# Attention of the shorter sequence in pairs of units: one maximum, one reciprocal and one copy for two

## What is computed

```python
sc = einsum('bqhcd,bkhcd->bhcqk', q_blk, k)      # c = 0, 1: two score maps for each head
p = softmax(sc, axis=-1)
w = p[:, :, 0] - lam * p[:, :, 1]
o = einsum('bhqk,bkhe->bqhe', w, v)              # then an RMSNorm over each head's 128 columns
```

## Time and profile before

| | |
|---|---|
| median of 3 runs | 2004.49 us (2004.25 to 2005.94) |
| the profiled execution | 2006.16 us, span 2004.4 us |
| TensorE, DVE, ACT, GpSimd busy | 93%, 74%, 53%, 24% of the span |
| mean granted clock of TensorE | 0.966 of full speed |
| attention of the short sequence | from 863.7 to 931.1 us of the span |

### The profile page before, as it was taken

The page is one execution under the profiler, slowest core; times in us unless marked ns, Lnnn a source line. Parts: engine busy times, 40 slices in busy tenths (PEclk is TensorE's granted clock), DMA queues, the critical chain, the costliest instruction groups (busy, mean ns, idle before and its releaser), DMA issues.

```text
span 2004.4 us, 31667 instructions
## 1 busy us (share of the span) xinstructions
PE 1871.2 (93%) x11554; PEld 1667.6 (83%) x11554; DVE 1480.8 (74%) x2246; ACT 1061.6 (53%) x1528; POOL 487.5 (24%) x366
## 2 busy tenths in 40 slices
PE   6999998998899989987995999999999999999995
PEld 6888876887579988766795999999999999999994
DVE  5335877996877568976757777877777777877786
ACT  4233337885671433375633555556555555556564
POOL 3444333221860133332501100111111100111110
PEclk9999999998999989988987999999999999999998
DMA  5332320000023423300335777777777777777886
GB/s 204 102 120 100 107 77 33 1 1 1 22 71 151 176 87 112 98 12 1 116 128 209 228 243 260 242 265 258 261 246 245 237 243 263 243 261 263 284 276 243
DMA packets 62755, 325.13 MB, mean 162 GB/s; under 512 B 8336, under 2 KB 14608, under 8 KB 32464
## 3 DMA queue, kind: packets, MB, share of 16 engines
q1 hardware_dynamic: 46640, 265.55, 37.3%
q0 software_dynamic: 16032, 58.47, 9.9%
HBM read 287.55 MB, written 34.87 MB: 161 GB/s over the span
## 4 chain that ended last, share of the span: by engine, by line
PE 76%; DVE 13%; ACT 5%; issue 4%; POOL 1%; DMA 1%; SPq 0%; POOLq 0%; DVEq 0%; ACTq 0%
PE psum L2386 20%; PE psum L1973 9%; PE psum L2387 9%; PE psum L1975 9%; PE psum L1974 9%; DVE conv_acc L1423 3%; PE psum L2409 3%; PE psum L2408 3%; PE psum L2124 3%; PE psum L2103 2%; PE psum L2112 1%; PE psum L2104 1%; PE psum L2240 1%; ACT prob L984 1%; PE psum L2328 1%
## 5 line engine op out<-in xcount | busy, mean ns | idle before, releaser
L2386 PE MATMUL psum<-xT,whi 128*128 128x384 f32 x1024 | 295.7, 361 | 1.3 <-DVE xT L1949 1.3
L2386 PE MATMUL psum<-xT,whi_x 128*128 128x384 f32 x1024 | 293.7, 360 | 0.0
L1878 DVE TENSOR_TENSOR wlo_x<-wraw_x,whi_x 128x2048 fp32r<-128x2048 f32 x96 | 218.4, 2288 | 59.0 <-ACT whi_x L1199 59.0
L2387 PE MATMUL psum<-xT,wlo 128*128 128x192 f32 x1024 | 257.8, 252 | 0.0
L2387 PE MATMUL psum<-xT,wlo_x 128*128 128x192 f32 x1024 | 256.8, 251 | 0.0
L1973 PE MATMUL psum<-ht_hi,whi 128*128 128x512 f32 (+1 forms) x624 | 238.6, 382 | 19.4 <-POOL wlo L597 7.0
L1975 PE MATMUL psum<-ht_hi,wlo 128*128 128x512 f32 (+1 forms) x624 | 236.0, 378 | 0.0
L1974 PE MATMUL psum<-ht_lo,whi 128*128 128x512 f32 (+1 forms) x624 | 235.9, 378 | 0.0
L1878 DVE TENSOR_TENSOR wlo<-wraw,whi 128x2048 fp32r<-128x2048 f32 x94 | 213.6, 2284 | 16.2 <-ACT whi L1199 16.2
L597 POOL TENSOR_TENSOR wlo<-wraw,whi 128x2048 fp32r<-128x2048 f32 x36 | 167.8, 4662 | 220.4 <-ACT whi L824 220.4
L2387 PEld LDWEIGHTS psum<-xT,wlo 128*128 128x128 f32 x1024 | 197.5, 193 | 0.6
(11 more groups left out here) (378 smaller groups left out, 4343.4 us busy)
## 6 DMA issues: line engine op xcount, KB each, us to landing
wraw<-moe_chunks SPq DMA_DIRECT2D x96, 1024.0 KB, 5.8
wraw_x<-moe_chunks SPq DMA_DIRECT2D x96, 1024.0 KB, 6.3
wraw<-w_in_chunks SPq DMA_DIRECT2D x36, 1024.0 KB, 4.9
wraw<-w_out_chunks SPq DMA_DIRECT2D x8, 1024.0 KB, 6.1
xin<-x POOLq DMA_DIRECT2D x12, 512.0 KB, 4.8
acc_scratch<-x POOLq DMA_DIRECT2D x12, 512.0 KB, 3.2
h_scratch<-h POOLq DMA_DIRECT2D x12, 512.0 KB, 3.9
fin<-acc_scratch SPq DMA_DIRECT2D x11, 512.0 KB, 11.3
```

Of the source, the lines that this page charges most:

```text
L1878: tt(moe_lo[i % 4], moe_raw[i % 4].rearrange("p (k n) -> p k n", k=KT), moe_hi[i % 4].bitcast(F32), ALU.subtract).then_inc(w_lo_done, 1)
L2386: mm(bank[:, 0:2 * TOK], hi[:, k, cols], xT[:, k, :], start=(k == 0), stop=False)
L2387: last = mm(bank[:, 0:TOK], lo[:, k, cols], xT[:, k, 0:TOK], start=False, stop=(k == KT - 1))
```

## The change

In the short sequence a step is now a pair of neighbouring units of one head (`each = 2`), 8 steps instead of 16; the long sequence is as before (`each = 1`). The helper `steps(s)` gives units in a step, number of steps, steps in a query block and steps in a head. A pair's two maps for c = 0 take both 512-column halves of the 1024 columns of PSUM that the long sequence uses, and so do those for c = 1.

A pair has one maximum of 128x1024 to 128x2 for each c, four exponentials of 512 columns as before (each has its own bias and its own sum), one reciprocal of four numbers, one small product for both units, two differences of 512 columns, eight transposes, one copy of 1024 columns, and the products of both units. A pair's semaphore for the scores comes after four matmuls, and the next pair's scores for c wait for both exponentials of that c.

The pieces of queries and keys are dealt out anew: the even pair of a head issues query pieces one and two, both low query pieces and both parts of the key, high and low; the odd pair issues query pieces three and four. GpSimd's low parts wait for `wg_done` only in the long sequence now. `scaled`, `squares` and `summed` come at other steps, and in the short sequence `squares` and `summed` of the last two blocks stand behind the loop, where only the last one did. `rsum` has 32 columns and another address. The dt steps keep their numbers, which now count pairs.

```diff
-        def q_low(u):
+        def q_low(s, u):
-            return (0, 1, None, None)[u % 4]
+            return ((0, 1) if u % 2 == 0 else ()) if s else ((0,), (1,), (), ())[u % 4]
+        def q_pieces(s, u):
+            if s:
+                return Q_PIECES[2 * (u % 2):2 * (u % 2) + 2]
             return (Q_PIECES[0:1], Q_PIECES[1:2], Q_PIECES[2:4], ())[u % 4]
-        def k_pieces(u, nt):
-            return [c_ for c_ in range(2) if u % nt == nt // 2 - 2 + c_]
+        def k_pieces(s, u):
+            return ((0, 1) if u % 2 == 0 else ()) if s else [c_ for c_ in range(2) if u % 8 == 2 + c_]
+        def steps(s):
+            each = 1 + s
+            return each, 4 * SEQS[s][1] // each, 4 // each, SEQS[s][1] // each
...
# GpSimd, k_lo and q_lo
-                        pool.wait_ge(wg_done, 4 * t0 + u + 1)
+                        if s == 0:
+                            pool.wait_ge(wg_done, u + 1)
...
# ACT
+                            for x_ in range(each):
+                                at_ = each * (2 * (u % 2) + c_) + x_
+                                act.activation(sl[:, c_, x_ * L:(x_ + 1) * L],
+                                               psum[:, 1024 * c_ + x_ * L:1024 * c_ + (x_ + 1) * L], ACT.Exp,
+                                               bias=ostat[:, 0, at_:at_ + 1], accum_out=ostat[:, 1, at_:at_ + 1]
+                                               ).then_inc(exp_done, 1)
-                        act.activation(wgtT[:, w % 2, 0:L], psum[:, 2048:2048 + L], ACT.Copy).then_inc(wt_out, 1)
+                        act.activation(wgtT[:, w % 2, :], psum[:, 2048:2048 + 1024], ACT.Copy).then_inc(wt_out, 1)
-                    if u // 4 + 1 < nt:
-                        q_hi(u // 4 + 1, q_pieces(u))
+                    if u // group + 1 < nt:
+                        q_hi(u // group + 1, q_pieces(s, u))
...
-                squares(act, s, nt - 1)
+                for a in range(nt - each, nt):
+                    squares(act, s, a)
...
# DVE
+                    own.link(dve.reciprocal(sums, ostat[:, 1, o2:o2 + 2 * each]))
+                    own.link(stt(out=ostat[:, 2, first], in0=ostat[:, 1, first], scalar=lamt[:, 6:7],
+                                 in1=sums[:, each:2 * each], op0=ALU.mult, op1=ALU.mult))
+                    for x_ in range(each):
+                        at_ = slice(x_ * L, (x_ + 1) * L)
+                        ins = stt(out=sl[:, 0, at_], in0=sl[:, 1, at_], scalar=ostat[:, 2, o2 + x_:o2 + x_ + 1],
+                                  in1=sl[:, 0, at_], op0=ALU.mult, op1=ALU.add)
+                    ins.then_inc(wg_done, 1)
...
+                            dve.tensor_reduce(ostat[:, 0, at_:at_ + each],
+                                              psum[:, 1024 * c_:1024 * c_ + 1024].rearrange("p (x l) -> p x l", x=each),
+                                              AX.X, ALU.max, negate=True).then_inc(mx_done, 1)
...
-                summed(nt - 1)
+                for a in range(nt - each, nt):
+                    summed(a)
...
# TensorE
+                            if u % group == 0:
+                                pe.wait_ge(qhi_done, 4 * (t0 + u // group) + c_ + 3)
+                                pe.wait_ge(qlo_done, 2 * (t0 + u // group) + c_ + 1)
...
                             if u:
-                                pe.wait_ge(exp_done, 2 * (U - 1) + c_ + 1)
-                            for q in range(L // BLK):
+                                pe.wait_ge(exp_done, 8 * t0 + each * (2 * (u - 1) + c_ + 1))
+                            for q in range(2):
+                                unit = each * u + (q if s else 0)
...
-                        for kk in range(nt):
+                        for kk in range(8):
                             last = pe.transpose(psum[:, 2048 + kk * P:2048 + (kk + 1) * P],
                                                 prob[s][w % 2][:, 0, kk * P:(kk + 1) * P], ident)
```

More of the change, by code:

```diff
@@ L625, in q_lo @@
                     h, i = (4 * a) // nt, (4 * a) % nt
[L626 to L633, removed]
+                    for c_ in q_low(s, u):
+                        if s == 0:
+                            pool.wait_ge(wg_done, u + 1)
+                        pool.wait_ge(qhi_done, 4 * (t0 + a) + Q_PIECES.index((c_, c_)) + 1)
+                        rows = slice(64 * c_, 64 * c_ + 64)
+                        pool.tensor_tensor(qhl[rows, a % 2, 2 + c_, :], qT[rows, h, i * P:i * P + BLK],
+                                           qhl[rows, a % 2, c_, :].bitcast(F32), ALU.subtract).then_inc(qlo_done, 1)
+                each, count, group, head = steps(s)
+                for u in range(count):
                     if u == 0:
@@ L638, in _ @@
                         pool.wait_ge(qlo_clear, 4 * s + 4)
[L639 to L642, removed]
+                    if u // group + 1 < nt:
+                        q_lo(u // group + 1, u)
+                    if u // head + 1 < HEADS:
+                        k_lo(u // head + 1, u)
                 pool.memset(mark[0:1, 1:2], 0.0).then_inc(phase_pool, 1)
@@ L975, in _ @@
                 use_table(ACT.Exp)
-                for u in range(4 * nt + 2):
+                each, count, group, head = steps(s)
+                for u in range(count + 2):
                     U = 4 * t0 + u
-                    if u < 4 * nt:
+                    if u < count:
                         sl = prob[s][u % 2]
@@ L1491, in dt_step @@
                         tt(grid(6), grid(5), rep(stat[:, 1, :]), ALU.mult).then_inc(dt_v, 1)
+                each, count, group, head = steps(s)
                 def weights(w):
                     W = 4 * t0 + w
-                    sl, o2 = prob[s][w % 2], 2 * (w % 2)
-                    dve.wait_ge(exp_done, 2 * W + 2)
-                    own.link(dve.reciprocal(rsum[:, 2 * (w % 8):2 * (w % 8) + 2], ostat[:, 1, o2:o2 + 2]))
-                    own.link(stt(out=ostat[:, 2, o2:o2 + 1], in0=ostat[:, 1, o2:o2 + 1],
-                                 scalar=rsum[:, 2 * (w % 8) + 1:2 * (w % 8) + 2], in1=lamt[:, 6:7],
-                                 op0=ALU.mult, op1=ALU.mult))
@@ L1502, in weights @@
-                    stt(out=sl[:, 0, 0:L], in0=sl[:, 1, 0:L], scalar=ostat[:, 2, o2:o2 + 1], in1=sl[:, 0, 0:L],
-                        op0=ALU.mult, op1=ALU.add).then_inc(wg_done, 1)
+                    sl, o2 = prob[s][w % 2], 2 * each * (w % 2)
+                    first = slice(o2, o2 + each)
+                    sums = rsum[:, 2 * each * (w % 8):2 * each * (w % 8 + 1)]
+                    dve.wait_ge(exp_done, 8 * t0 + 2 * each * (w + 1))
+                    own.link(dve.reciprocal(sums, ostat[:, 1, o2:o2 + 2 * each]))
@@ L1513, in summed @@
+                    r = rsum[:, at_:at_ + 8].rearrange("p (u c x) -> p u c x", c=2, x=each)[:, :, 0, :]
+                    tt(oatt[:, i:i + 4, h * P:(h + 1) * P].rearrange("p (u x) n -> p u x n", x=each),
+                       pb[6 + a % 2].rearrange("p (u x n) -> p u x n", x=each, n=P),
+                       r.unsqueeze(3).to_broadcast([P, group, each, P]), ALU.mult).then_inc(o_scaled, 1)
                 def summed(a):
@@ L2085, in _ @@
                 pe.wait_ge(rot_out, NR * (b + 1))
-                for u in range(4 * nt + 3):
+                each, count, group, head = steps(s)
+                for u in range(count + 3):
                     U = 4 * t0 + u
-                    if u < 4 * nt:
-                        h, i = u // nt, u % nt
+                    if u < count:
+                        h, i = u // head, u % head
                         for c_ in range(2):
```

79 lines of the change are left out of this document (35 added, 44 removed).

## The result

The changed kernel takes 2015.25 us, median of 5 runs (2013.64 to 2017.03), the kernel before 2005.19 us beside it, also 5 (2004.25 to 2005.98): 1.0050 times, with a 95% interval of 1.0035 to 1.0065. The prediction was 2013.5, range 2007.5 to 2018.5. The profiled execution took 2015.85 us, with a span of 2014.0 where before had 2004.4.

The account below looks back on a forecast made before the run. The prediction took a ring from ACT to TensorE and back, 2.80 us a unit, to bound the short attention. Its terms, 1.4 + 7.2 + 0.4 = 9.0 us on the median 2004.49, gave 2013.5 us, range 2007.5 to 2018.5.

Parts of the forecast that it names:

- The markers and the rest: Short attention's times, from first exponential 866.41 to last sum of squares 925.02; the change leaves what follows that alone.
- DVE's saving of 2.4 us at 0: Short attention: 32 maxima become 16, 2.4 us less DVE work, taken as worth 0, at most 2.4.
- the ring: Short attention's loop from ACT to TensorE and back to ACT, 2.80 us a unit, with DVE beside it.
- A free pair 5.05 us against 5.60: A short-attention pair without late waits takes 5.05 us against 5.60, one round of hand-overs for two; eight pairs 4.4 us.
- Three late waits: Scores of pairs 2, 4, 6 wait for ACT's late query copies; TensorE idles 4.7, up to 5 and 3 us.
- The walk at full clock, +1.4 us: Pair-by-pair start times at TensorE's full clock, through the tail: the last sum ends at 926.4, 1.4 us later than 925.02.
- The clock, 7.2 us and 0.4 for the products: Clock falls before pairs 2, 4, 6: 2.4 us each on scores and transposes, 7.2; products 0.4, bounds 0 and 4.8.
- GpSimd and DVE at 0: GpSimd's low halves run into DVE's differences after even pairs: about 2.5 us, hidden by slack, taken as 0, at most 4.
- Rival C: GpSimd and DVE hold each other, key's low halves late: 4 us more, low-clock products 4.8 more, 2017.5 to 2022; chance 0.11.
- Rival A: The waits are there, but TensorE's clock falls at most once: 1.4 to 4 us, 2006 to 2008.5; chance 0.17.
- Rival B: Late pieces come before TensorE asks, each pair gains 0.55 us: 4.4 less the tail's extra, at most -4, 2000.5; chance 0.04.
- The sum of 9.0 us: Predicted total loss: 1.4 from the walk plus 7.2 from the clock, 8.6, and 0.4 for the products.

Follow-up runs that it names:

- e1_even: Changed kernel with all four query pieces of the next head copied in the even pair, none in the odd one: 2008.36 us, ratio 1.0015 to before.
- e4_ahead: Changed kernel with the query pieces dealt one pair earlier, each later pair keeping its count of copies: 2005.20 us, ratio 0.9997 to before.
- e2_fill: Changed kernel with unused small identity matmuls before the scores of pairs 1, 2, 4 and 6, where TensorE idled: 2008.80 us, ratio 1.0022 to before.
- e3_poolwait: Changed kernel with GpSimd's wait for `wg_done` put back ahead of the short sequence's low halves: 2019.66 us, ratio 1.0069 to before.
- e10_atail: e4_ahead with the copy of pair 5's weights ahead of the last pair's exponentials, no small matmuls or early table load: 2003.71 us, ratio 0.9994.
- e7_afill: e4_ahead plus the exponential's table loaded right behind the logarithm and small identity matmuls before the scores of pairs 1 and 2: 2005.85 us, ratio 0.9998.
- e8_tail: e7_afill with ACT's copy of pair 5's weights ahead of the last pair's four exponentials, not behind them: 2000.12 us, ratio 0.9974 to before.
- e12_again: The kernel of e8_tail run once more, nothing else changed: 1999.93 us, ratio 0.9973 to before.

## Why the prediction was right, and where it was off

- **The markers and the rest.** All of the loss is in the stage, none of it in the rest (1945.4 and 1945.8).
- **DVE's saving of 2.4 us at 0.** Maxima of 1223 ns, DVE behind TensorE in the waits of the changed kernel, and no version shows a gain from it alone. But its ground, that the ring hides DVE, was not so in the first units of before: ACT waited 4.4 us for DVE's maxima, 2.71 of them ahead of unit 2. Not tested by itself.
- **A free pair 5.05 us against 5.60.** Pair 6 took 5.0 (48.0 to 53.0). Shown.
- **Three late waits.** 4.37, 4.33 and 3.94 us, against 4.7, up to 5 and 3. e1_even and e4_ahead took them away, and 7.0 and 10.6 us with them. Shown; the third was a little longer than forecast.
- **The walk at full clock, +1.4 us.** With the clock held (e2_fill) it is 61.6 against 60.0 predicted. The step that failed is "The reload of the exponential's table, another 1.28, fits beside TensorE's 3.1": it stood behind them, since the load starts only when the exponential's own wait is over (the 4.11 us above). Pair 4 was 1.3 us late by it, in e2_fill and after.
- **The clock, 7.2 us and 0.4 for the products.** 5.6 to 7.0 us measured, but otherwise dealt: the steps of after less those of e2_fill are 2.2 us at pair 2 (8.8 and 6.6), 0.3 at pair 3, 1.6 at pair 4 (12.0 and 10.4), 1.2 at pair 6 (9.1 and 7.9) and 1.6 in the tail (15.5 and 13.9), 7.0 together. At pair 6 the clock fell only at 911.7, one microsecond into the scores. In the tail it was the sixteen products, where the sum had 0.4 for all products. The term came out right in part by luck: the three falls that it priced at 7.2 were worth 5.1, and the two that it left out gave 1.9. "I take a fall at each" held, but there were five falls, and a walk that puts falls only at the longest idlings misses the one of the tail, after 2.15 us. No walk by idle times alone could place it, for e2_fill and e4_ahead idled as long there without a fall.
- **GpSimd and DVE at 0.** The timeline bears it out (2.8 us of slack behind the first held differences), and the hold is 1.98 us on two differences (3.39 less 1.41), where the walk had about 2.5. Rival C needed scores waiting on `khl` more than on `qhl`. In the scores' weight loads that came when the wait was put back (e3_poolwait) or the query wait was gone (e1_even, e4_ahead); it set the scores' start only in e3_poolwait.
- **Rival A**, 2006 to 2008.5 with the clock held: e2_fill is that case by force, 2008.8, just above it.
- **Rival B**, the hand-overs decide at 2000.5 when the pieces are early: e4_ahead made them early and came to 2005.2. Up to pair 7 there were 3.2 us of its 4.4, all from the first two pairs, and they were lost in the tail, which B's sum had as "4.4 less the tail's extra, at most -4": the tail's extra was 3 us (13.9 against 10.9), and should have been taken off. To reach 2000.1 it took the early copy, the small matmuls and the early load together; with the early copy alone (e10_atail) it is 2003.7.

The sum of 9.0 us stands against 9.95 in the stage and 10.1 in the medians: 1.3 by the table, 0.3 by small shifts, less 0.6 by the clock as a whole. The mechanism was right, the late query copies and the clock behind them; that the total comes so close is owed in part to errors of opposite sign.

## What to carry to other kernels

When two units are joined into one, every piece of preparation that was spread over the units must be put again: look at which instruction in an in-order queue stands behind the last piece, and for how many units' worth of work it is. Price the deeper pipeline's tail apart from its loop: with the pieces early, pair 7 started 3.2 us sooner and the tail gave 3.0 back. One copy moved ahead of four exponentials in the last pair then gave about 1 us by its order, and with small matmuls against the low clock beside it the kernel came below the one before; without them it was level (0.9994, interval 0.9983 to 1.0005). Here a wait that kept two engines from holding each other cost more than it saved, because the matmuls waited for what it delayed (e3_poolwait).

## What the runs showed of the hardware

- The length of an idling alone does not tell whether the clock falls. e7_afill and e8_tail are the same up to the last pair, with the same idlings of 2.44 us before pair 3 and 2.72 us before pair 5, some 1 us shifted; in one profiled execution the clock fell at both, in the other at none, nor in that of e12_again, the same kernel as e8_tail. First e7_afill, then e8_tail, 878 to 884 and 892 to 896:

```profile
878.00:884.00 6.00, 4.21 (x15) 3.28 (x16) 4.94 (x9) 5.64 (x13) 0.36 (x1) 0.72 0.00 1
...
892.00:896.00 4.00, 1.75 (x4) 1.46 (x5) 3.63 (x9) 3.95 (x11) 2.52 (x2) 0.73 0.00 0
```
```profile
878.00:884.00 6.00, 3.44 (x20) 2.35 (x18) 4.93 (x9) 4.69 (x12) 1.27 (x2) 1.00 0.01 1
...
892.00:896.00 4.00, 1.28 (x8) 0.99 (x7) 3.90 (x7) 3.94 (x11) 2.52 (x2) 1.00 0.00 0
```

- The pairs of those two start at the same times up to pair 6 (38.3 and 38.4 us) all the same: there ACT and not TensorE set the pace, and the low clock cost nothing.
- A table load that belongs to an exponential is issued after that exponential's waits: 4.11 us idle ahead of the load at 898.79, and 1.28 us on the path of pair 4.
- A two-input subtraction of GpSimd and a two-input difference of DVE hold each other: 3.39 us for two that take 1.41 alone, and GpSimd's two took 2.93 us beside them where they take 2.60 without (e3_poolwait). A DVE operation with one tensor input is held as well: in the kernel before, the step on 128x64 at 871.43 (L1475) took 1.28 us beside GpSimd, and another of its kind (L1483) 0.19 us alone.
